# Second mixer of a hybrid encoder layer: where the next head's queries and keys are turned, when they are copied out, and reciprocals of two tiles at a time

## The chip, the cores and the metric

The kernel runs on one core of a Trainium2 chip. The metric is the time of one execution on the device, in microseconds (us), over the whole layer. A lower number is better. Three runs of the kernel before are shown, and one execution taken by the hardware profiler.

Engine names in the profile: PE is TensorE's matmul side, PEld its weight loads, DVE is VectorE, ACT is ScalarE, POOL is GpSimd, SP is SyncE, which issues the DMAs.

## The reference

One encoder layer over 2048 tokens of width 1024. The input projection feeds two mixers: A is grouped-query attention, B a dilated sliding-window attention with 8 heads of width 64. Their outputs are normalised, joined and projected; an MLP and a gated addition follow. The change lies in mixer B:

```
DILATED_PATTERNS = ((128, 1), (512, 4), (2048, 16))
    sc = einsum('brnqhd,brnkhd->brnqhk', qs, ks) * (HEAD_DIM ** -0.5)
    sc = where(valid, sc + bias, NEG_BIG)
    mx = max(sc, axis=-1)
    e = exp(sc - mx[..., None])
    den = sum(e, axis=-1)
    o = einsum('brnqhk,brnkhd->brnqhd', e, vs) / den[..., None]
```

The three patterns are merged by their softmax denominators. The kernel treats the union of the patterns' keys of a tile of queries as one softmax, with a table of biases that also holds the counts of keys that several patterns share and the masks.

## The kernel before

The layer is a chain of phases: projection, mixer A, mixer B (`mixer_b_phase`), and the feed phase with output projection, MLP and gate. Each phase is a block with its own program per engine, and a barrier stands between two. Semaphores order the engines inside a block; each engine runs its own program strictly as written, so the order in the code is the order of the work.

Mixer B loops over heads, two per turn of the hardware loop (`Fori`, `par` 0 and 1), and over NU = 16 tiles of 128 queries in each, n = 0 to 15. N counts tiles over all heads. Scores of a tile are 128 x 1024 at most: eight blocks of 128 keys, of which the first is left out where n mod 4 is 0 or 3, so that some tiles have seven. Every number is split in a high and a low float part for TensorE's faster float format, hence the pairs "hi" and "lo".

What one iteration N does on each engine:

- TensorE (from L1257): in iterations n = 2 to 9, `prepare(h + 1, n - 2)` (L1188): four transposes that turn one of eight blocks of the next head's queries or keys into the accumulator bank `out_acc[n % 2]`. Then `scores(N + 2)` (L1203, L1210, L1216), `turn(N + 1)` (L1226), which turns the probabilities, `fold_out(N + 1)` (L1248), which turns tile N - 1's sums back, and `values(N)` (L1240), which writes `out_acc[n % 2]`.
- ScalarE: `turned_hi(N + 1)` (L1307, two halves), `exponential(N + 2)` (L1300), in iterations n = 1 to 8 `pre_out(h + 1, n - 1)` (L1291), which copies the turned block out of its bank into `pre`, then `sums_out(N)` (L1313).
- VectorE: `add_bias(N + 2)` (L1362, three parts, and the maximum, L1365), `output` of tile N - 1 (L1382), which multiplies with the reciprocal of the denominator, `sums(N + 1)` (L1377), that reciprocal, and `turned_lo(N + 1)` (L1372, two halves).
- GpSimd: splits `pre` into high and low parts of the next head's queries and keys (`split_pre`, L1126 to L1133), adds parts of outputs (`summed`, L1148, L1153), splits the next head's values (`split_values`) and copies its bias tables (`tables`, L1104 to L1113), in this order.
- SyncE: loads of the next head's inputs and tables, stores of the outputs.

The waits that the change and the prediction speak of: `prepare` waits for `y_done`, which `output` raises, since it writes the bank that `output` of tile n - 2 has read. `values` waits for `y_done`, for `lo_done`, and in iterations 2 to 9 for `pre_raw`, which `pre_out` raises:

```
                pe.wait_ge(lo_done, N * 2 + 2)
                pe.wait_ge(y_done, N + 1)
                if 2 <= n < 2 + PRE:
                    pe.wait_ge(pre_raw, h * PRE + (n - 1))
```

`scores(N + 2)` waits only for `add_done` of tile N, whose bank it takes. `turn(N + 1)` waits for `exp_done`.

Of the kernel before, what the change touches and what calls it, by code (L numbers as in the profile page):

```python
# [969 lines left out]
def mixer_b_phase(nc, scr, step, ident, heads, feed, consts, chunks):  # L970
# [11 lines left out]
    SLOTS = 4  # L982
    with ExitStack() as ctx:
        k = Kit(nc, ctx, "mixb")
# [11 lines left out]
        den = k.sb("den", [P, SLOTS])  # L996
        rden = k.sb("rden", [P, SLOTS])
# [15 lines left out]
                                                                            "v_hi", "v_lo"))  # L1013
        sc_done, add_done, nm_done, exp_done = (k.sem(n) for n in ("sc_done", "add_done", "nm_done", "exp_done"))
        t_done, hi_done, lo_done, pv_done = (k.sem(n) for n in ("t_done", "hi_done", "lo_done", "pv_done"))
        rd_done, o_done, fold_done, y_done = (k.sem(n) for n in ("rd_done", "o_done", "fold_done", "y_done"))
        y_ready = k.sem("y_ready")
        y_out = k.sems("y_out", 2)
        QK_DMAS, V_DMAS = heads.QK_DMAS, heads.V_DMAS
# [1 line left out]
        PRE = 8  # L1021
# [156 lines left out]
        def _(pe):  # L1178
            def prepare(h, m):

                if m == 0:
                    pe.wait_ge(qk_dma, h * (16 * QK_DMAS) + 16 * QK_DMAS)
                first = isinstance(h, int)
                if first and m >= 6:
                    pe.wait_ge(pre_lo, m - 5)
                src = q_in if m < 4 else k_in
                for j in range(4):
                    mm = pe.transpose(pre_banks[m % (6 if first else 2)][:, j * P:(j + 1) * P],  # L1188
                                      src[:, 4 * (m % 4) + j, :], ident[:])
                mm.then_inc(pre_done, 1)  # L1190

            def scores(N, par, n):

                r, b = n // RES, n % RES
                if not (isinstance(N, int) and N < 2):
                    pe.wait_ge(add_done, N * 3 - 3)
                sc = score[n % 2]
                q = qT[par][:, n * P:(n + 1) * P]
                for part in range(2):
                    kt = kT[par][part]  # L1200
                    main = kt[:, PAD:PAD + S].rearrange("p (r m) -> p r m", r=RES)
                    own = first_own(n)
                    pe.matmul(sc[:, first_tile(n) * P:BANK], q, main[:, r, own * P:(own + RES - first_tile(n)) * P],  # L1203
                              start=part == 0, stop=part == 1)
                at = BANK
                runs = [x for x in ((0, r), (r + 1, RES)) if x[1] > x[0]]
                for a, z in runs:
                    for part in range(2):
                        main = kT[par][part][:, PAD:PAD + S].rearrange("p (r m) -> p r m", r=RES)
                        pe.matmul(sc[:, at:at + (z - a) * P], q, main[:, a:z, b * P:(b + 1) * P],  # L1210
                                  start=part == 0, stop=part == 1)
                    at += (z - a) * P
                for part in range(2):
                    t = kT[par][part][:, b * P:b * P + PAD]
                    ends = bass.AP(t.tensor, t.offset, [[SW, P], [SUB, RES], [P + PAD, 2], [1, PAD]])
                    mm = pe.matmul(sc[:, at:at + P], q, ends, start=part == 0, stop=part == 1)  # L1216
                mm.then_inc(sc_done, 1)

            def turn(N, n):
                pe.wait_ge(exp_done, N + 1)  # L1220
                for half in range(2):
                    if not (isinstance(N, int) and N == 0):
                        pe.wait_ge(lo_done, N * 2 + half - 1)
# [36 lines left out]
            with pe.Fori(0, NHB // 2) as it:  # L1260
                for par in range(2):
                    h = it * 2 + par
                    for n in range(NU):
                        N = h * NU + n
                        if 2 <= n < 2 + PRE:
                            pe.wait_ge(y_done, N + 1)
                            prepare(h + 1, n - 2)
                        if n < NU - 2:
                            scores(N + 2, par, n + 2)
                        else:  # L1270
                            if n == NU - 2:
                                pe.wait_ge(pre_lo, h * PRE + 2 * PRE)
                                pe.wait_ge(v_lo, h + 2)
                            scores(N + 2, 1 - par, n + 2 - NU)
                        turn(N + 1, (n + 1) % NU)
                        fold_out(N + 1, n - 1)
                        values(N, h, par, n)
            fold_out(NHB * NU + 1, NU - 1)

        @block.scalar  # L1280
        def _(act):
            def pre_hi_part(h, par, m):
                act.wait_ge(pre_done, h * PRE + m + 1)
                dst = qT[par][:, m * BANK:(m + 1) * BANK] if m < 4 else kT[par][0][:, PAD + (m - 4) * BANK:
                                                                               PAD + (m - 3) * BANK]
                act.activation(dst, pre_banks[m % 6], ACT.Copy).then_inc(pre_hi, 1)

            def pre_out(h, m):
                act.wait_ge(pre_done, h * PRE + m + 1)
                act.wait_ge(pre_lo, h * PRE + m - 1)  # L1290
                act.activation(pre[:, m % 2, :], out_acc[m % 2][:], ACT.Copy).then_inc(pre_raw, 1)  # L1291

            def value_hi(h, par):
                act.wait_ge(v_dma, h * (16 * V_DMAS) + 16 * V_DMAS)
                act.activation(v_hl[par][:, :, 0:HD], v_in[:], ACT.Copy).then_inc(v_hi, 1)

            def exponential(N, n):
                act.wait_ge(nm_done, N + 1)
                p = prob[:, n % SLOTS, first_tile(n) * P:]
                act.activation(p, p, ACT.Exp, bias=nmax[:, n % SLOTS:n % SLOTS + 1],  # L1300
                               accum_out=den[:, n % SLOTS:n % SLOTS + 1]).then_inc(exp_done, 1)

            def turned_hi(N, n):
                for half in range(2):
                    act.wait_ge(t_done, N * 2 + half + 1)
                    j = 0 if half else first_tile(n)
                    act.activation(pT[:, n % 2, 4 * half + j:4 * half + 4, 0, :],  # L1307
                                   turned[half][:, j * P:].rearrange("p (c n) -> p c n", n=P), ACT.Copy
                                   ).then_inc(hi_done, 1)

            def sums_out(N, n):
                act.wait_ge(pv_done, N + 1)
                act.activation(oT[:, n % 2, :], out_acc[n % 2][:, 0:2 * P], ACT.Copy).then_inc(o_done, 1)  # L1313

            for m in range(PRE):
                pre_hi_part(0, 0, m)
            exponential(0, 0)
            value_hi(0, 0)
            exponential(1, 1)
            turned_hi(0, 0)  # L1320
            with act.Fori(0, NHB // 2) as it:
                for par in range(2):
                    h = it * 2 + par
                    for n in range(NU):
                        N = h * NU + n
                        turned_hi(N + 1, n + 1)
                        exponential(N + 2, n + 2)
                        if 1 <= n < 1 + PRE:
                            pre_out(h + 1, n - 1)
                        sums_out(N, n)  # L1330

        @block.vector
        def _(ve):
# [38 lines left out]
                    ve.tensor_tensor(at[:, :, 1, :], turned[half][:, j * P:].rearrange("p (c n) -> p c n", n=P),  # L1372
                                     at[:, :, 0, :].bitcast(F32), ALU.subtract).then_inc(lo_done, 1)

            def sums(N, n):
                ve.wait_ge(exp_done, N + 1)
                ve.reciprocal(rden[:, n % SLOTS:n % SLOTS + 1], den[:, n % SLOTS:n % SLOTS + 1]).then_inc(rd_done, 1)  # L1377

            def output(count, n):

# [8 lines left out]
            add_bias(0, 0, 0)  # L1389
            add_bias(1, 0, 1)  # L1390
            value_lo(0, 0)
            sums(0, 0)
            turned_lo(0, 0)
            with ve.Fori(0, NHB // 2) as it:
                for par in range(2):
                    h = it * 2 + par
                    for n in range(NU):
                        N = h * NU + n
                        if n < NU - 2:
                            add_bias(N + 2, par, n + 2)  # L1400
                        else:
                            if n == NU - 2:
                                ve.wait_ge(t_done_pool, h * T_COPIES + 2 * T_COPIES)
                            add_bias(N + 2, 1 - par, n + 2 - NU)
                        if n % 2 == 1:
                            ve.wait_ge(y_ready, h * 16 + (n // 2 * 2 + 1))
                        output(N + 1, (n - 1) % NU)
                        sums(N + 1, n + 1)
                        turned_lo(N + 1, n + 1)
            output(NHB * NU + 1, NU - 1)  # L1410

# [805 lines left out]
```

## Time and profile before

| what | value |
|---|---|
| median of three runs | 3624.57 us (3621.48 to 3624.72) |
| profiled execution | 3623.18 us |
| its span, first to last instruction | 3621.4 us |
| mean granted TensorE clock | 0.975 of full speed |
| PE matmul / PEld busy over the span | 3418.6 (94%) / 2881.5 us (80%) |
| DVE / ACT / POOL busy | 2455.4 (68%) / 1892.9 (52%) / 2061.3 us (57%) |

The busy times are sums over all phases. Matmuls are pipelined and their ends are modelled, so a busy PE does not mean that it is at its peak. In a timeline, the distance between the starts of two neighbours on an engine is the step of the first; the duration may be longer, since neighbours overlap. The value in brackets is the idle time of the engine ahead of the instruction and what ended it.

### The profile page before, as it was taken

How to read it: one execution, taken by the hardware profiler on the slowest of the kernel's cores; microseconds unless marked ns; L12 is line 12 of the kernel's file. 1: busy time of each engine (PE TensorE's matmuls, PEld its weight loads, DVE VectorE, ACT ScalarE, POOL GpSimd, SP SyncE). 2: the span in 40 equal slices, each digit the busy share in tenths (PEclk: the TensorE clock that was granted, in tenths of full speed). 3: DMA queues.
4: the chain of work that ended last, by engine and by line, in shares of the span. 5: the costliest groups of instructions: out<-in, count | busy, mean ns of one | idle time of the engine just before them, and what ended most of it. 6: DMA issues, size and time to landing. Idle time of an engine off the chain costs nothing.

```text
span 3621.4 us, 55821 instructions
## 1 busy us (share of the span) xinstructions
PE 3418.6 (94%) x17910; PEld 2881.5 (80%) x17910; DVE 2455.4 (68%) x4319; ACT 1892.9 (52%) x3554; POOL 2061.3 (57%) x1416
## 2 busy tenths in 40 slices
PE   7999989999999899998699998999989999899997
PEld 6888868888888788888478886888868888778885
DVE  5555579999999788888355576555665556655554
ACT  3222268888888677777343353433543345433342
POOL 4555424443222265655467775677766777657773
PEclk9999989999999999999799999999999999999998
DMA  4545434443002233334234444444443444434441
GB/s 178 164 163 175 138 125 153 146 147 109 17 17 50 61 65 82 77 71 111 87 106 156 146 137 148 139 151 152 140 155 126 153 155 145 157 112 150 146 151 53
DMA packets 289135, 444.91 MB, mean 123 GB/s; under 512 B 175412, under 2 KB 194300, under 8 KB 282908
## 3 DMA queue, kind: packets, MB, share of 16 engines
q1 hardware_dynamic: 279580, 428.48, 38.0%
q10 hardware_dynamic: 9344, 13.73, 1.0%
q8 instruction: 119, 1.95, 0.2%
q14 instruction: 92, 0.75, 0.1%
HBM read 377.89 MB, written 76.71 MB: 126 GB/s over the span
## 4 chain that ended last, share of the span: by engine, by line
PE 42%; DVE 6%; ACT 2%; issue 1%; POOL 0%; DMA 0%; SPq 0%; DVEq 0%; ACTq 0%
PE feed_bank L1668 41%; DVE feed_res L1976 2%; DVE feed_total L1973 1%; DVE feed_xn L1949 1%; ACT feed_xT L1826 1%; PE feed_bank L1659 1%; DVE feed_xT L1958 0%; POOL feed_w_split L1619 0%; DVE feed_ms L1937 0%; DMA feed_y_in<-scr_yB 0%; DVE feed_total L2033 0%; DVE feed_rec L1940 0%; DVE feed_comb L2060 0%; ACT feed_junk L1801 0%; DVE feed_sums L2079 0%
## 5 line engine op out<-in xcount | busy, mean ns | idle before, releaser
L1619 POOL TENSOR_TENSOR feed_w_split<-feed_w_raw,feed_w_split 128x1024 fp32r<-128x1024 f32 x424 | 1077.9, 2551 | 254.6 <-ACT feed_w_split L1854 235.7
L1668 PE MATMUL feed_bank<-feed_w_split,feed_comb 128*128 128x512 f32 x3648 | 855.0, 395 | 28.0 <-DVE feed_sums L2079 10.4
L1668 PEld LDWEIGHTS feed_bank<-feed_w_split,feed_comb 128*128 128x128 f32 x3648 | 690.8, 190 | 181.2 <-DVE feed_sums L2079 12.9
L1668 PE MATMUL feed_bank<-feed_xT,feed_w_split 128*128 128x512 f32 x3072 | 700.7, 390 | 2.5 <-DVE feed_xT L1958 2.5
L1668 PEld LDWEIGHTS feed_bank<-feed_xT,feed_w_split 128*128 128x128 f32 x3072 | 577.5, 188 | 123.2 <-DVE feed_xT L1958 2.9
L1616 POOL TENSOR_SCALAR feed_w_split<-feed_w_raw 128x1024 fp32r<-128x1024 f32 x200 | 228.9, 1145 | 323.4 <-issue 306.5
L357 PE MATMUL proj_bank<-proj_w_split,proj_xT 128*128 128x512 f32 (+1 forms) x1920 | 402.5, 370 | 2.7 <-issue 2.7
L952 DVE TENSOR_TENSOR mixa_pT<-mixa_turned,mixa_pT 128x512 fp32r<-128x512 f32 x512 | 350.9, 685 | 58.4 <-ACT mixa_pT L898 50.1
L357 PEld LDWEIGHTS proj_bank<-proj_w_split,proj_xT 128*128 128x128 f32 x1920 | 333.3, 189 | 66.8 <-issue 5.6
L898 ACT ACTIVATE mixa_pT<-mixa_turned 128x512 fp32r<-128x512 f32 x512 | 307.1, 600 | 123.1 <-PE mixa_turned L836 104.1
L795 PE MATMUL mixa_out_acc<-mixa_pT,mixa_v_hl 128*128 128x512 f32 x1028 | 366.0, 437 | 0.7 <-DVE mixa_pT L952 0.7
L2033 DVE TENSOR_TENSOR feed_total<-feed_total,feed_bank 128x512 f32<-128x512 f32 x352 | 224.4, 681 | 195.7 <-PE feed_bank L1668 192.7
L1869 ACT ACTIVATE feed_rl<-feed_bank 128x512 f32<-128x512 f32 x128 | 76.5, 598 | 523.2 <-PE feed_bank L1668 523.2
L1854 ACT ACTIVATE feed_w_split<-feed_w_raw 128x1024 fp32r<-128x1024 f32 x224 | 236.6, 1065 | 189.8 <-PE feed_bank L1668 185.1
L923 DVE TENSOR_REDUCE mixa_nmax<-mixa_score 128x1 f32<-128x1024 f32 x264 | 322.0, 1221 | 14.3 <-PE mixa_score L782 7.7
L836 PE MATMUL mixa_turned<-layer_ident,mixa_prob 128*128 128x128 f32 x2048 | 307.7, 273 | 0.0
L836 PEld LDWEIGHTS mixa_turned<-layer_ident,mixa_prob 128*128 128x128 f32 x2048 | 253.1, 141 | 56.3 <-issue 0.2
L870 ACT ACTIVATE mixa_prob<-mixa_score,mixa_nmax 128x1024 f32<-128x1024 f32 x263 | 294.2, 1119 | 4.0 <-DVE mixa_nmax L923 4.0
L782 PE MATMUL mixa_score<-mixa_kT,mixa_qT 128*128 128x512 f32 x1056 | 289.1, 395 | 7.0 <-ACT mixa_prob L870 6.2
L2002 DVE TENSOR_TENSOR feed_comb<-feed_rl,feed_comb 128x256 fp32r<-128x256 f32 x128 | 154.0, 1203 | 174.5 <-ACT feed_comb L1873 174.2
L782 PEld LDWEIGHTS mixa_score<-mixa_kT,mixa_qT 128*128 128x128 f32 x1056 | 198.6, 189 | 55.8 <-ACT mixa_prob L870 8.7
L1668 PE MATMUL feed_bank<-feed_w_split,feed_xT 128*128 128x512 f32 x768 | 185.4, 402 | 9.5 <-ACT feed_total L1833 7.1
(198 smaller groups left out, 5101.9 us busy)
## 6 DMA issues: line engine op xcount, KB each, us to landing
feed_w_raw<-w_tail_dram SPq DMA_DIRECT2D x200, 512.0 KB, 3.6
feed_w_raw<-scr_wT SPq DMA_DIRECT2D x160, 512.0 KB, 3.3
proj_w_raw<-w_in_dram SPq DMA_DIRECT2D x39, 1024.0 KB, 5.2
feed_w_raw<-w_ff_dram SPq DMA_DIRECT2D x64, 512.0 KB, 3.5
scr_table<-scr_bias SPq DMA_DIRECT2D x8, 1520.0 KB, 9.0
proj_x_t<-x_dram SPq DMA_DIRECT2D x20, 512.0 KB, 5.8
mixa_q_in<-scr_qA SPq DMA_DIRECT2D x36, 256.0 KB, 3.4
mixb_q_in<-scr_qB SPq DMA_DIRECT2D x18, 512.0 KB, 5.7
```

Source lines behind the costliest of these rows:

```text
L357: mm = pe.matmul(acc[t][:, 0:width], xT[u][a][:, k0 + kk, t * P:(t + 1) * P], w[m][:, kk, :], start=first and kk == 0 and q == 0, stop=las ...
L782: mm = pe.matmul(score[:, at * BANK:(at + 1) * BANK], qT[g][:, h, :], kT[g][part][:, kc * BANK:(kc + 1) * BANK], start=part == 0, stop=par ...
L795: mm = pe.matmul(out_acc[half][:], v_hl[:, s, g, :], pT[part][:, s % NR, :], start=s % (NT // 2) == 0 and part == 0, stop=s % (NT // 2) == ...
L836: mm = pe.transpose(turned[s % 2][:, h * P:(h + 1) * P], prob[w][:, h, s * P:(s + 1) * P], ident[:])
L870: act.activation(prob[par][:, h, half * 2 * BANK:(half + 1) * 2 * BANK], score[:, 2 * (c % 2) * BANK:2 * (c % 2 + 1) * BANK], ACT.Exp, bia ...
L898: act.activation(pT[0][:, s % NR, :], turned[s % 2][:], ACT.Copy).then_inc(hi_done, 1)
L923: ve.tensor_reduce(nmax[:, par, c // G, c % G:c % G + 1], score[:, 2 * (c % 2) * BANK: 2 * (c % 2 + 1) * BANK], AXX, ALU.max, negate=True) ...
L952: ve.tensor_tensor(pT[1][:, s % NR, :], turned[s % 2][:], pT[0][:, s % NR, :].bitcast(F32), ALU.subtract).then_inc(lo_done, 1)
L1616: pool.tensor_scalar(w_sp[0][:, slot, :], w_raw[:, slot, :], 1.0, 0.0, ALU.mult, ALU.add).then_inc(w_hi, 1)
L1619: pool.tensor_tensor(w_sp[1][:, slot, :], w_raw[:, slot, :], w_sp[0][:, slot, :].bitcast(F32), ALU.subtract).then_inc(w_lo, 1)
L1668: mm = pe.matmul(dst, lhs, rhs, start=start, stop=stop)
L1854: act.activation(w_sp[0][:, slot, :], w_raw[:, slot, :], ACT.Copy).then_inc(w_hi_ff, 1)
```

## The change

Three edits, all in `mixer_b_phase`. On TensorE `prepare` and its wait for `y_done` move behind `scores(N + 2)`, in the same iterations. On ScalarE `pre_out` moves from the place between `exponential` and `sums_out` to the head of the following iteration, ahead of `turned_hi`. On VectorE the reciprocal is taken for two tiles at a time, in even iterations, and the one ahead of the loop and its semaphore `rd_done`, for which nobody waited, go.

```diff
@@ TensorE's loop
                     for n in range(NU):
                         N = h * NU + n
-                        if 2 <= n < 2 + PRE:
-                            pe.wait_ge(y_done, N + 1)
-                            prepare(h + 1, n - 2)
                         if n < NU - 2:
                             scores(N + 2, par, n + 2)
                         else:
@@
                             scores(N + 2, 1 - par, n + 2 - NU)
+                        if 2 <= n < 2 + PRE:
+                            pe.wait_ge(y_done, N + 1)
+                            prepare(h + 1, n - 2)
                         turn(N + 1, (n + 1) % NU)
@@ ScalarE's loop
+                        if 2 <= n < 2 + PRE:
+                            pre_out(h + 1, n - 2)
                         turned_hi(N + 1, n + 1)
                         exponential(N + 2, n + 2)
-                        if 1 <= n < 1 + PRE:
-                            pre_out(h + 1, n - 1)
                         sums_out(N, n)
@@ VectorE
-            def sums(N, n):
+            def sums_of_two(N, n):
+
+                at = slice(n % SLOTS - 1, n % SLOTS + 1)
                 ve.wait_ge(exp_done, N + 1)
-                ve.reciprocal(rden[:, n % SLOTS:n % SLOTS + 1], den[:, n % SLOTS:n % SLOTS + 1]).then_inc(rd_done, 1)
+                ve.reciprocal(rden[:, at], den[:, at])
@@
-            sums(0, 0)
             turned_lo(0, 0)
@@ VectorE's loop
-                        sums(N + 1, n + 1)
+                        if n % 2 == 0:
+                            sums_of_two(N + 1, n + 1)
                         turned_lo(N + 1, n + 1)
```

TensorE, the iteration n = 8 of the first head of a loop turn (`mixb_k_in` is the next head's keys, `mixb_prob` the probabilities, `mixb_oT` the sums to be turned back). Before:

```order
L1188 MATMUL mixb_out_acc<-layer_ident,mixb_k_in 128x128 x4
L1196 ISA
L1203 MATMUL mixb_score<-mixb_kT,mixb_qT 128x512 x2
L1210 MATMUL mixb_score<-mixb_kT,mixb_qT 128x256 x2
L1210 MATMUL mixb_score<-mixb_kT,mixb_qT 128x128 x2
L1216 MATMUL mixb_score<-mixb_kT,mixb_qT 128x128 x2
L1223 ISA
L1226 MATMUL mixb_turned<-layer_ident,mixb_prob 128x128 x8
L1248 MATMUL mixb_out_acc<-layer_ident,mixb_oT 128x128 x2
L1235 REGISTER_ALU
L1238 REGISTER_ALU
L1240 MATMUL mixb_out_acc<-mixb_pT,mixb_v_hl 128x256 x7
```

The same iteration in the changed kernel:

```order
L1196 ISA
L1203 MATMUL mixb_score<-mixb_kT,mixb_qT 128x512 x2
L1210 MATMUL mixb_score<-mixb_kT,mixb_qT 128x256 x2
L1210 MATMUL mixb_score<-mixb_kT,mixb_qT 128x128 x2
L1216 MATMUL mixb_score<-mixb_kT,mixb_qT 128x128 x2
L1188 MATMUL mixb_out_acc<-layer_ident,mixb_k_in 128x128 x4
L1223 ISA
L1226 MATMUL mixb_turned<-layer_ident,mixb_prob 128x128 x8
L1248 MATMUL mixb_out_acc<-layer_ident,mixb_oT 128x128 x2
L1235 REGISTER_ALU
L1238 REGISTER_ALU
L1240 MATMUL mixb_out_acc<-mixb_pT,mixb_v_hl 128x256 x7
```

The four transposes of L1188 stood ahead of the scores and now stand between the scores and the turning.

ScalarE, a `prepare` iteration in the middle of a head. Between two exponentials, before:

```order
L1300 ACTIVATE mixb_prob,mixb_den<-mixb_prob,mixb_nmax 128x1024
L1289 REGISTER_ALU
L1291 ACTIVATE mixb_pre<-mixb_out_acc 128x512
L1313 ACTIVATE mixb_oT<-mixb_out_acc 128x256
L1305 ISA
L1307 ACTIVATE mixb_pT<-mixb_turned 128x4x128
```

And now:

```order
L1300 ACTIVATE mixb_prob,mixb_den<-mixb_prob,mixb_nmax 128x1024
L1313 ACTIVATE mixb_oT<-mixb_out_acc 128x256
L1289 REGISTER_ALU
L1291 ACTIVATE mixb_pre<-mixb_out_acc 128x512
L1305 ISA
L1307 ACTIVATE mixb_pT<-mixb_turned 128x4x128
```

The copy L1291 has changed places with L1313; it now stands directly ahead of the first half of the turned probabilities.

## Rows read from the trace of the kernel before

**Rows 1.** Windows of mixer B, their sum: TensorE matmuls, loads, VectorE, ScalarE, GpSimd.

```profile
sum 463.00, PE 433.36 PEld 408.16 DVE 392.51 ACT 357.56 POOL 257.87; mean PE 108.34 PEld 102.04 DVE 98.13 ACT 89.39 POOL 64.47
```

**Rows 2.** Waits of TensorE's weight loads, 1250 to 1712: us, times, longest.

```profile
PEld mixb_out_acc L1188 <- DVE mixb_y_part L1382: 26.2, 56, 0.9
...
PEld mixb_out_acc L1188 <- issue: 1.0, 3, 0.3
```

**Rows 3.** Timeline, TensorE, n = 8: start, us, engine, line, what, [idle before].

```profile
1517.52 0.66 PE L1188 MATMUL mixb_out_acc<-layer_ident,mixb_k_in 128*128 128x128 f32 x4 [0.41 <-DVE mixb_y_part L1382]
1517.93 0.70 PE L1203 MATMUL mixb_score<-mixb_kT,mixb_qT 128*128 128x512 f32 x2
...
1519.10 1.06 PE L1226 MATMUL mixb_turned<-layer_ident,mixb_prob 128*128 128x128 f32 x8
1520.00 0.38 PE L1248 MATMUL mixb_out_acc<-layer_ident,mixb_oT 128*128 128x128 f32 x2
1520.13 1.08 PE L1240 MATMUL mixb_out_acc<-mixb_pT,mixb_v_hl 128*128 128x256 f32 x7
1521.48 0.66 PE L1188 MATMUL mixb_out_acc<-layer_ident,mixb_k_in 128*128 128x128 f32 x4 [0.27 <-DVE mixb_y_part L1382]
```

**Rows 4.** Timeline, VectorE, the same iteration.

```profile
1519.46 0.69 DVE L1362 CUSTOM_DVE_ANT_0 mixb_prob<-mixb_score,mixb_t_own 128x512 f32<-128x512 f32 x1 [0.87 <-PE mixb_score L1216]
...
1520.95 0.47 DVE L1382 TENSOR_SCALAR mixb_y_part<-mixb_out_acc,mixb_rden 128x256 f32<-128x256 f32 x1
1521.35 0.15 DVE L1377 RECIPROCAL mixb_rden<-mixb_den 128x1 f32<-128x1 f32 x1
1521.42 1.27 DVE L1372 TENSOR_TENSOR mixb_pT<-mixb_turned,mixb_pT 128x512 fp32r<-128x512 f32 x2
```

**Rows 5.** Timeline, VectorE, iterations n = 12 to 14, first bias of each.

```profile
1532.54 0.68 DVE L1362 CUSTOM_DVE_ANT_0 mixb_prob<-mixb_score,mixb_t_own 128x512 f32<-128x512 f32 x1
...
1535.68 0.56 DVE L1362 CUSTOM_DVE_ANT_0 mixb_prob<-mixb_score,mixb_t_own 128x384 f32<-128x384 f32 x1
...
1538.84 0.56 DVE L1362 CUSTOM_DVE_ANT_0 mixb_prob<-mixb_score,mixb_t_own 128x384 f32<-128x384 f32 x1
```

**Rows 6.** Timeline, TensorE, turning of iteration n = 12.

```profile
1532.49 1.09 PE L1226 MATMUL mixb_turned<-layer_ident,mixb_prob 128*128 128x128 f32 x8 [0.35 <-ACT mixb_prob L1300]
```

**Rows 7.** Timeline, first `prepare` of a head: TensorE, ScalarE, GpSimd.

```profile
1493.99 0.65 PE L1188 MATMUL mixb_out_acc<-layer_ident,mixb_q_in 128*128 128x128 f32 x4
...
1494.76 0.60 ACT L1291 ACTIVATE mixb_pre<-mixb_out_acc 128x512 f32<-128x512 f32 x1 [0.16 <-PE mixb_out_acc L1188]
...
1495.56 0.62 POOL L1126 TENSOR_SCALAR mixb_qT<-mixb_pre 128x512 fp32r<-128x512 f32 x1 [4.35 <-ACT mixb_pre L1291]
```

**Rows 8.** Timeline, TensorE behind ScalarE's last copy.

```profile
1714.37 0.36 ACT L1313 ACTIVATE mixb_oT<-mixb_out_acc 128x256 f32<-128x256 f32 x1
...
1714.78 0.44 PE L1248 MATMUL mixb_out_acc<-layer_ident,mixb_oT 128*128 128x128 f32 x2 [1.43 <-ACT mixb_oT L1313]
```

**Rows 9.** Timeline, ScalarE, iteration n = 8.

```profile
1519.76 1.09 ACT L1307 ACTIVATE mixb_pT<-mixb_turned 128x512 fp32r<-128x512 f32 x2 [0.68 <-PE mixb_turned L1226]
1521.07 1.15 ACT L1300 ACTIVATE mixb_prob<-mixb_prob,mixb_nmax 128x1024 f32<-128x1024 f32 x1 [0.22 <-DVE mixb_nmax L1365]
...
1522.22 0.58 ACT L1291 ACTIVATE mixb_pre<-mixb_out_acc 128x512 f32<-128x512 f32 x1
1522.70 0.37 ACT L1313 ACTIVATE mixb_oT<-mixb_out_acc 128x256 f32<-128x256 f32 x1
```

**Rows 10.** Timeline, GpSimd, the last copy of the next head's tables.

```profile
1535.06 0.24 POOL L1113 COPY mixb_t_end<-mixb_t_near 128x64 f32<-128x64 f32 x1
```

**Rows 11.** Instructions on the reciprocals' tile: ns min/median/max, first and last start.

```profile
L1377 DVE RECIPROCAL mixb_rden<-mixb_den x129: 151/154/157, 1252.9 to 1713.5; 128x1 f32<-128x1 f32 x129
```

**Rows 12.** Timeline, ScalarE, the first work of the next phase.

```profile
1719.76 0.63 ACT L1817 ACTIVATE feed_junk<-feed_total 128x512 bf16<-128x512 f32 x1 [5.02 <-PEq L983]
```

More of the change, by code:

```diff
@@ L1015, in mixer_b_phase @@
         t_done, hi_done, lo_done, pv_done = (k.sem(n) for n in ("t_done", "hi_done", "lo_done", "pv_done"))
-        rd_done, o_done, fold_done, y_done = (k.sem(n) for n in ("rd_done", "o_done", "fold_done", "y_done"))
+        o_done, fold_done, y_done = (k.sem(n) for n in ("o_done", "fold_done", "y_done"))
         y_ready = k.sem("y_ready")
```

## The prediction

> **What bounds the kernel now.** I read the stretches of time first. Mixer B runs from about 1250 to 1713 us of the 3621.4 us span. In these 463 us TensorE's matmuls are busy 433, VectorE 393, ScalarE 358 and GpSimd 258 [rows 1]: TensorE is the fullest, VectorE the next. Nothing outside this stretch is touched.
>
> Then the waits of TensorE's weight loads there [rows 2]. The largest is ahead of L1188, `prepare`, the turning of the next head's queries and keys: 26.2 us in 56 waits for VectorE's `output` (L1382), and 1.0 us in 3 more laid to issue. There are 64 `prepare` in the loop (8 heads, 8 each), so 59 of 64 wait, 0.46 us each.
>
> The timeline shows why. One iteration of n = 8 on TensorE [rows 3]: `prepare` starts at 1517.52, scores 1517.93, turning 1519.10, folding 1520.00, values 1520.13, next `prepare` 1521.48, a period of 3.96. VectorE starts on those scores at 1519.46, 0.36 after TensorE went on to turning; it had been idle 0.87 before [rows 4]. It reaches `output` at 1520.95, ends it at 1521.42, and TensorE starts the next `prepare` 0.06 later. So a loop closes in these iterations: scores, bias, output, `prepare`, next scores. Both engines idle in it. `prepare` needs that output only because it writes the accumulator bank that the output reads; the scores behind it need nothing of it.
>
> In the other 8 iterations of a head there is no `prepare`. VectorE starts at 1532.54, 1535.68 and 1538.84, 3.14 and 3.16 apart [rows 5], nearly without a gap. There VectorE sets the pace, now and then the exponential: one turning waits 0.35 for it [rows 6].
>
> **The change part by part.**
>
> *Scores ahead of `prepare`.* Scores may start when values are issued. `prepare` then comes 1.17 later (the scores' step, 1517.93 to 1519.10 [rows 3]). Is the output ready by then? It ends 0.36 + 1.49 + 0.47 = 2.32 after the end of the scores before (1519.10 to 1519.46, to 1520.95, to its end [rows 3, 4]); the next `prepare` comes one period, some 3.6, after that. Slack 1.3. The wait goes whole. Not all of it is idle time: the seven value matmuls take (1.08 - 0.28)/6 = 0.133 each, so they are issued by 1520.13 + 0.93 = 1521.06, and the 0.42 to 1521.48 stands in the trace as 0.47 of the load unit's idle time. I take 0.03 off each: 27.2 - 59 x 0.03 = 25.4 us gained. The work of such an iteration is then 3.96 - 0.44 = 3.52.
>
> *A wait that takes its place.* `values` waits for `pre_raw`, the copy of the turned block out of the bank (L1291 on ScalarE), since it writes that bank. Before, scores lay between `prepare` and `values`; now only turning and folding do. Counted from the start of `prepare`: the copy starts 0.77 later when ScalarE is waiting for it (1493.99 to 1494.76), takes 0.60 [rows 7], and its end is seen after 0.05 (TensorE behind L1313: 1714.37 + 0.36 to 1714.78 [rows 8]) to 0.20 (GpSimd: 1495.36 to 1495.56 [rows 7]). Values can start at 1.42 to 1.57. TensorE is there at 0.41 + 0.90 + 0.13 = 1.44 (the steps of `prepare`, turning and folding) with eight blocks to turn [rows 3], and some 0.11 earlier in the half of the iterations with seven. The stall is 0 to 0.13 with eight and 0.09 to 0.24 with seven: 0.045 to 0.185 on average. I take 0.07, near the low end, because the row with 0.05 is TensorE's own wait for ScalarE. 64 x 0.07 = 4.5 us lost (bounds 2.9 and 12).
>
> This is where a rule and the rows part. The Trainium skill ("TensorE: Matmul & The Clock Gate", step-by-step phases) says that TensorE pulls weight loads ahead of matmuls in flight. Read as reaching across a semaphore wait, it would hide the restart and bring this stall to about nothing. The rows speak against that reach: behind a wait the loads idle at least as long as the matmuls (26.2 us of load idle time stands before L1188 [rows 2]).
>
> *The copy ahead of the turned probabilities.* ScalarE now does copy, two `turned_hi`, exponential, `sums_out`. The copy starts at 0.77 and holds the engine 0.48 (1522.22 to 1522.70 [rows 9]), so `turned_hi` starts at 1.25. Without it, it would start at 0.41 + 0.66 = 1.07 (1519.10 to 1519.76 [rows 3, 9]). It is 0.18 late, some 0.3 with seven blocks. Who waits? The exponential follows at 1.25 + 1.09 = 2.34; its input is ready at about 0.36 + 1.61 = 1.97 (1519.46 to 1521.07 [rows 4, 9]). It is done at 2.34 + 1.15 = 3.49, and the next turning wants it at 3.6 + 0.41 = 4.0. `turned_lo` ends near 3.7 and is wanted at 5.0. `sums_out` frees ScalarE at 3.9, and the next copy starts at 4.3. All have slack, the least about 0.4, so I cost this at nothing. When that cover is gone each 0.1 us is 6.4 us.
>
> *GpSimd and the queues.* The splits of the copied blocks begin about 1.1 us later in an iteration. The next head's tables are behind them on GpSimd: their last copy ends at 1535.30 [rows 10], while VectorE wants them at 1538.84 [rows 5]. 3.5 us of slack become some 2.4. Nothing, and SP's loads start as much later with a whole half head to land.
>
> *Reciprocals of two tiles.* Of 129 L1377 [rows 11] 65 go, one of them ahead of the loop. Each is 0.15 long, but its step is 0.07 (1521.35 to 1521.42 [rows 4]): 4.5 us less VectorE work. Half of it falls in `prepare` iterations, where VectorE idles. Of the other 2.2 us a part goes to the waits for the exponential. I take 1.0 (bounds 0 and 4.5).
>
> *Behind the mixer.* The next phase starts behind the last store, at 1719.76, after an idle time that ends at the barrier [rows 12]. It shifts with the mixer.
>
> **Sum.** 25.4 - 4.5 + 1.0 = 21.9 us. The profiled execution took 3623.18, so 3601.3; the median of the three runs, 3624.57, is 1.4 above it: **3602.7 us**.
>
> **The rivals.**
>
> *The new wait is hidden too.* Stall zero, reciprocals paid to 2.2: 27.6 us, 3597 us. For it: with eight blocks TensorE arrives at 1.44 against 1.42. Against: with seven it arrives early by any of the rows. Chance 0.10. The rule on pulled loads, above, would lead here.
>
> *ScalarE's order takes the gain.* If `turned_hi` is on the path after all, 0.18 to 0.3, say 0.23, comes on each of 64 iterations: 14.7 us, 7.2 left, 3617 us. For it: a period near 3.6 rests on four hand-overs whose slack is 0.4. Against: the walk above. Chance 0.10. The Trainium skill (same page, on queue depths) calls ScalarE's queue a strict FIFO, so nothing passes a copy that waits; if the copy waited for `prepare` longer than I count, this rival is how it would show.
>
> *VectorE is the bound in these iterations too*, so that nearly nothing is won: its work is 3.14 to 3.16 [rows 5] against 3.6, so it would need a slip of 0.5. 3624 us. Chance 0.04.
>
> *Slower: the copy comes late.* TensorE stands at `values` with all next scores queued behind it. ScalarE is in order, so the copy starts only when the exponential and `sums_out` of the iteration before are through, at 3.9 against 4.3. It decides from 0.4 of slip on, and the change loses once the stall passes 0.42 per iteration, the wait removed. With a slip of 0.9, a stall of 0.57: 64 x 0.57 = 36 lost against 26 won, 3635 us. For it: the copy is now first in ScalarE's iteration. Against: ScalarE is busy only 358 of 463 us [rows 1]. Chance 0.04.
>
> **Numbers.** The forecast has 0.72. What a measurement of this kernel can tell from no change is about 0.2%, 7 us. Range: bounds give 25.4 - 2.9 + 4.5 = 27 at best (3597.6) and 25.4 - 12 = 13.4 at worst (3611.2). I widen it to 3596 to 3613 for the first rival and part of the second. Faster by over 0.2%: 0.72 + 0.10 + half of the second rival = 0.87. Within: 0.09. Slower: 0.04.
>
> **What would show it.** Right: no wait of L1188 for L1382 left; a new small wait of L1240 for L1291, under 0.25 each, longer where seven blocks are turned; VectorE starts 3.5 to 3.7 apart in `prepare` iterations and near 3.1 in the others; mixer B shorter by 20 to 24 us, all else shifted. Wrong: waits of L1240 over 0.3; turning waiting for the exponential in `prepare` iterations; VectorE without idle time there; or a tail that does not shift.

## The result, and the profile after

The changed kernel takes 3593.44 us (four runs, 3591.33 to 3594.26) against 3623.53 us (four runs) before: a ratio of 0.9917, 95% interval 0.9899 to 0.9934. That is 30.1 us less. The direction and the wait that goes were forecast; the size was not, nor that the forecast new wait would stay away. 21.9 us were expected, and the time lies 2.6 us below the range. The profiled execution took 3593.50 us.

The head of the page of the changed kernel, and the line of TensorE's granted clock over the 40 slices:

```profile
span 3591.7 us, 55756 instructions
...
PE 3406.2 (95%) x17910; PEld 2881.9 (80%) x17910; DVE 2454.1 (68%) x4254; ACT 1878.5 (52%) x3554; POOL 2058.2 (57%) x1416
...
PEclk9999989999999999998799999999999999999998
```

The clock is as before (0.974 on average against 0.975). The instructions are the same but for 65 reciprocals. The sum over mixer B, the window 1250 to 1682:

```profile
sum 432.00, PE 417.95 PEld 405.96 DVE 391.33 ACT 344.32 POOL 256.94; mean PE 417.95 PEld 405.96 DVE 391.33 ACT 344.32 POOL 256.94
```

Set beside [rows 1], 463 us have become 432 with the same work in them but for the reciprocals: VectorE's busy time fell by 1, the weight loads' by 2. Idle time went, and a few steps of TensorE became shorter (told with why the prediction was wrong). Two busy figures fell by more, and neither by less work. ScalarE's fell by 13, while its instructions last as long as before (L1307 571 ns on average against 570, L1291 599 against 589): records that follow each other closely overlap, as 1500.25 + 0.60 and 1500.75 below, and the overlap counts once. TensorE's fell by 15; it is made of modelled ends, and a group is drawn longer behind a wait (L1188 0.66 in [rows 3], 0.62 below), which explains some of it; the rest was not taken apart.

All waits of TensorE's weight loads of 1 us and more, from 1250 to 1685, so that the last folding of the mixer is in (us, times, longest). They answer to [rows 2]:

```profile
PEld mixb_score L1203 <- issue: 7.6, 3, 2.8
PEld mixb_turned L1226 <- issue: 6.0, 24, 0.3
PEld mixb_turned L1226 <- DVE mixb_v_hl L1347: 4.8, 1, 4.8
PEld mixb_out_acc L1248 <- ACT mixb_oT L1313: 1.6, 1, 1.6
PEld mixb_turned L1226 <- DVE mixb_pT L1372: 1.0, 2, 0.5
```

No row of L1188 for L1382 is left, and no row of L1240 for L1291 has come. The first was forecast; the second was not: the view lists no wait of `values` for the copy. One iteration n = 8 on TensorE, the counterpart of [rows 3]:

```profile
1498.50 0.62 PE L1203 MATMUL mixb_score<-mixb_kT,mixb_qT 128*128 128x512 f32 x2
...
1499.59 0.62 PE L1188 MATMUL mixb_out_acc<-layer_ident,mixb_k_in 128*128 128x128 f32 x4
1500.05 1.04 PE L1226 MATMUL mixb_turned<-layer_ident,mixb_prob 128*128 128x128 f32 x8
1500.93 0.38 PE L1248 MATMUL mixb_out_acc<-layer_ident,mixb_oT 128*128 128x128 f32 x2
1501.06 1.08 PE L1240 MATMUL mixb_out_acc<-mixb_pT,mixb_v_hl 128*128 128x256 f32 x7
1501.98 0.51 PE L1203 MATMUL mixb_score<-mixb_kT,mixb_qT 128*128 128x384 f32 x2
```

The order is scores, `prepare`, turning, folding, values. The period is 1498.50 to 1501.98, 3.48 instead of 3.96. ScalarE beside it, the counterpart of [rows 9]:

```profile
1499.37 0.39 ACT L1313 ACTIVATE mixb_oT<-mixb_out_acc 128x256 f32<-128x256 f32 x1
1500.25 0.60 ACT L1291 ACTIVATE mixb_pre<-mixb_out_acc 128x512 f32<-128x512 f32 x1 [0.50 <-PE mixb_out_acc L1188]
1500.75 1.08 ACT L1307 ACTIVATE mixb_pT<-mixb_turned 128x512 fp32r<-128x512 f32 x2
1501.70 1.16 ACT L1300 ACTIVATE mixb_prob<-mixb_prob,mixb_nmax 128x1024 f32<-128x1024 f32 x1
...
1502.83 0.39 ACT L1313 ACTIVATE mixb_oT<-mixb_out_acc 128x256 f32<-128x256 f32 x1
```

The copy L1291 starts 0.66 after `prepare`, ends at 1500.85, and the values start at 1501.06. The two turned halves (L1307) start 0.70 behind the turning, where it was 0.66 before ([rows 3, 9]: 1519.10 to 1519.76) with eight blocks; with seven it is 0.70 against 0.55. So they are late by 0.04 and 0.15, forecast were 0.18 and 0.3, and TensorE's steps show nobody waiting for that.

VectorE's first bias at the ends of one run of `prepare` iterations and one run without. After, iterations n = 10, then n = 2, then n = 10 of the next head:

```profile
1506.70 0.56 DVE L1362 CUSTOM_DVE_ANT_0 mixb_prob<-mixb_score,mixb_t_own 128x384 f32<-128x384 f32 x1 [0.23 <-PE mixb_score L1216]
...
1531.45 0.56 DVE L1362 CUSTOM_DVE_ANT_0 mixb_prob<-mixb_score,mixb_t_own 128x384 f32<-128x384 f32 x1 [0.22 <-PE mixb_score L1216]
...
1558.82 0.56 DVE L1362 CUSTOM_DVE_ANT_0 mixb_prob<-mixb_score,mixb_t_own 128x384 f32<-128x384 f32 x1 [0.23 <-PE mixb_score L1216]
```

Before, n = 9, n = 1 and n = 9. The run begins one iteration earlier there because `prepare` stood ahead of the scores:

```profile
1523.32 0.56 DVE L1362 CUSTOM_DVE_ANT_0 mixb_prob<-mixb_score,mixb_t_own 128x384 f32<-128x384 f32 x1 [0.63 <-PE mixb_score L1216]
...
1548.06 0.55 DVE L1362 CUSTOM_DVE_ANT_0 mixb_prob<-mixb_score,mixb_t_own 128x384 f32<-128x384 f32 x1
...
1579.00 0.56 DVE L1362 CUSTOM_DVE_ANT_0 mixb_prob<-mixb_score,mixb_t_own 128x384 f32<-128x384 f32 x1 [0.63 <-PE mixb_score L1216]
```

Eight iterations with `prepare`: 1531.45 to 1558.82, 27.37 us, against 30.94 (1548.06 to 1579.00). That is 3.42 for one, a little under the 3.5 to 3.7 that the prediction named as its sign. Eight without: 24.75 against 24.74. So it is 3.57 us per head where `prepare` is, and nothing elsewhere. Eight heads make 28.6; a further 1.5 us come from four `prepare` iterations in the whole mixer that took 0.37 longer than their like before (4.23 from values to values against 3.86) and no longer do.

The next phase starts at 1688.98 instead of 1719.76 [rows 12], 30.8 earlier. The profiled executions as a whole differ by 29.7, so about 1 us of that is lost again behind the mixer:

```profile
1688.98 0.63 ACT L1819 ACTIVATE feed_junk<-feed_total 128x512 bf16<-128x512 f32 x1 [5.03 <-PEq L983]
```

### The profile page after: what moved, and what is told of

Same layout as the page of the kernel before. It is cut to its first block, busy times and chain, and to the rows that moved or that the text cites. A ratio compares the mean times of both kernels' runs of the same rounds, so it can differ in the third digit from the quotient of the medians.

```text
span 3591.7 us, 55756 instructions
## 1 busy us (share of the span) xinstructions
PE 3406.2 (95%) x17910; PEld 2881.9 (80%) x17910; DVE 2454.1 (68%) x4254; ACT 1878.5 (52%) x3554; POOL 2058.2 (57%) x1416
## 4 chain that ended last, share of the span: by engine, by line
PE 42%; DVE 6%; ACT 2%; issue 1%; POOL 0%; DMA 0%; SPq 0%; DVEq 0%; ACTq 0%
PE feed_bank L1670 42%; DVE feed_res L1978 2%; DVE feed_total L1975 1%; DVE feed_xn L1951 1%; ACT feed_xT L1828 1%; PE feed_bank L1661 1%; DVE feed_xT L1960 0%; POOL feed_w_split L1621 0%; DVE feed_ms L1939 0%; DMA feed_y_in<-scr_yB 0%; DVE feed_rec L1942 0%; DVE feed_total L2035 0%; DVE feed_comb L2062 0%; ACT feed_junk L1803 0%; DVE feed_sums L2081 0%
```

## The experiments

Theory A: the wait of `prepare` for the output is the whole gain, and the swap on ScalarE only keeps a new wait away. The rivals: B, ScalarE has slack enough for either order; C, the swap gains by itself; D, the reciprocals explain what came over the forecast. The first four kernels take the parts one by one, each against the kernel before. A run's name stands in brackets at its result, and it is used further down.

### Only `prepare` behind the scores

```diff
@@ kernel before, TensorE's loop
-                        if 2 <= n < 2 + PRE:
-                            pe.wait_ge(y_done, N + 1)
-                            prepare(h + 1, n - 2)
@@ behind scores(N + 2, ...)
+                        if 2 <= n < 2 + PRE:
+                            pe.wait_ge(y_done, N + 1)
+                            prepare(h + 1, n - 2)
```

> Only prepare moves behind the scores on TensorE; ScalarE's order and the reciprocals stay as before. Theory A (the removed wait for the output is the whole gain, and the swap on ScalarE only keeps a new wait away): the copy now waits for prepare with the copy of the sums (L1313) queued behind it, so folding (L1248) stalls. From the changed kernel's trace the copy starts 0.66 after prepare; 0.66 + 0.48 + 0.38 + 0.05 = 1.57 against a folding that is due 1.22 to 1.34 after prepare: 0.23 to 0.35 in each of 64 iterations, 15 to 22 us. Expected 3608 to 3616, prepare iterations about 3.7 apart. Rival B (ScalarE has slack enough for either order): 3593 to 3596, no wait of L1248.

Measured (e_pe): 3625.44 us against 3624.13, ratio 1.0002 (0.9993 to 1.0012). All of the gain is gone, which is more than either theory gave: theory A had 3608 to 3616. The wait in question, TensorE's loads ahead of folding, from 1250 to 1680 (24.9 us in 64 waits over the whole mixer):

```profile
PEld mixb_out_acc L1248 <- ACT mixb_oT L1313: 23.1, 59, 0.5
```

Iteration n = 8, TensorE, then the two copies on ScalarE:

```profile
1518.49 0.62 PE L1188 MATMUL mixb_out_acc<-layer_ident,mixb_k_in 128*128 128x128 f32 x4
1518.95 1.04 PE L1226 MATMUL mixb_turned<-layer_ident,mixb_prob 128*128 128x128 f32 x8
1520.07 0.44 PE L1248 MATMUL mixb_out_acc<-layer_ident,mixb_oT 128*128 128x128 f32 x2
1520.37 1.09 PE L1240 MATMUL mixb_out_acc<-mixb_pT,mixb_v_hl 128*128 128x256 f32 x7
1521.29 0.51 PE L1203 MATMUL mixb_score<-mixb_kT,mixb_qT 128*128 128x384 f32 x2
```

```profile
1519.15 0.60 ACT L1291 ACTIVATE mixb_pre<-mixb_out_acc 128x512 f32<-128x512 f32 x1 [1.03 <-PE mixb_out_acc L1188]
1519.64 0.38 ACT L1313 ACTIVATE mixb_oT<-mixb_out_acc 128x256 f32<-128x256 f32 x1
```

The copy of the turned block (L1291) starts 0.66 after `prepare`, the copy of the sums (L1313) stands behind it and ends at 1520.02, and folding starts at 1520.07. It was due at 1518.95 + 0.88 = 1519.83. That is the 0.24 that theory A expected here. But folding itself then takes 1520.07 to 1520.37, 0.30, where it takes 0.13 in the stream (1500.93 to 1501.06 above). So the wait costs 0.41 here, not 0.24. Over all 64 `prepare` iterations the step of the turning is 1.14 on average against 0.82 in the changed kernel, 0.32 more, and that of folding 0.32 against 0.14, 0.18 more. 64 x 0.50 = 32 us, and the two kernels differ by 3625.44 - 3593.44 = 32.0. Theory A thus had the first part right and lacked the second. Rival B falls: ScalarE's order decides.

### Only the swap on ScalarE

```diff
@@ kernel before, ScalarE's loop
+                        if 2 <= n < 2 + PRE:
+                            pre_out(h + 1, n - 2)
                         turned_hi(N + 1, n + 1)
                         exponential(N + 2, n + 2)
-                        if 1 <= n < 1 + PRE:
-                            pre_out(h + 1, n - 1)
                         sums_out(N, n)
```

> Only the copy moves on ScalarE, which in fact swaps it with the copy of the sums (L1313) and nothing else; TensorE's order as before. Theory A: nobody waits for either in this place, so no change, 3621 to 3626. Rival C (part of the 30 us comes from ScalarE releasing the sums earlier): 3610 to 3618.

Measured (e_act): 3624.07 against 3624.13 us, ratio 1.0000 (0.9990 to 1.0010). The wait for the output stands as it did, up to 1680 us (before, up to there, 24.8 in 53):

```profile
PEld mixb_out_acc L1188 <- DVE mixb_y_part L1382: 24.5, 52, 0.9
```

Rival C falls. Each of the two moves alone is worth nothing, and together they are worth 30 us.

### Only the reciprocals

The edit is the third part of the change, on the kernel before.

> Only the reciprocals of two tiles at a time. Theory A: at most the half of 4.5 us that falls where VectorE sets the pace, so 3621.5 to 3624.5, and the eight iterations without prepare 24.6 to 24.8 us together against 24.8. Rival D (the reciprocals explain what came over the forecast): 3616 to 3620.

Measured (e_recip): 3621.14 against 3624.13 us, ratio 0.9995 (0.9985 to 1.0005): not told apart from no change (the ratio of the two medians is 0.9992, within the interval too). The output's wait is a little smaller, up to 1680 us (before 24.8 in 53):

```profile
PEld mixb_out_acc L1188 <- DVE mixb_y_part L1384: 23.3, 53, 0.6
```

The 1.5 us between them are the four longer iterations named above: they are gone here too (the last section comes back to them).

### Both moves without the reciprocals

The first two parts of the change on the kernel before.

> Both moves without the reciprocals. Theory A: within 1.5 us of the changed kernel, 3593 to 3596. Rival D: 3597 to 3600.

Measured (e_pe_act): 3594.08 us, ratio 0.9916 (0.9899 to 0.9932). It was run once more beside the changed kernel on one chip:

> The changed kernel once more, beside the other two on one chip: 3591 to 3595.

> The two moves without the reciprocals once more, beside the changed kernel on one chip. In the earlier traces the eight iterations without prepare took 24.83 us against 24.74 with the reciprocals, so 0.7 us over the changed kernel, which the times can hardly show; 2 us or more would mean that the reciprocals act elsewhere too.

Measured (a_after, e_norecip): 3592.28 us (ratio 0.9914, 0.9900 to 0.9927) with the reciprocals of two, 3593.30 us (0.9918, 0.9905 to 0.9932) without. The difference of 1.0 us is within the scatter. Rival D falls: the reciprocals bring at most about 1 us here, and the runs cannot tell it from nothing.

### The copy behind the turned probabilities

```diff
@@ changed kernel, ScalarE's loop
-                        if 2 <= n < 2 + PRE:
-                            pre_out(h + 1, n - 2)
                         turned_hi(N + 1, n + 1)
+                        if 2 <= n < 2 + PRE:
+                            pre_out(h + 1, n - 2)
```

> The changed kernel with the copy behind the two turned_hi instead of ahead of them. If values (L1240) truly waits for the copy, it starts 1.04 (when turned_hi starts) + 1.0 = 2.0 to 2.1 after prepare instead of 0.66, ends at 2.7, and values, due at 1.36 to 1.46, stalls 1.25 each: some 80 us, 3670 to 3680. If something else releases the bank earlier, or ScalarE's order does not matter: under 3600.

Measured (e_copy_late): 3675.24 us in one run, within the range, against 3622.71 before and 82 above the changed kernel's 3593.44. The wait that the forecast had feared is now there, up to 1680 us (78.2 in 64 over the whole mixer):

```profile
PEld mixb_out_acc L1240 <- ACT mixb_pre L1291: 67.1, 55, 1.2
```

So the dependence is real, and the place ahead of `turned_hi` is needed.

### The copy twice

```diff
@@ changed kernel, pre_out; spare is a tile of its own
+                act.activation(spare[:], out_acc[m % 2][:], ACT.Copy)
                 act.activation(pre[:, m % 2, :], out_acc[m % 2][:], ACT.Copy).then_inc(pre_raw, 1)
```

> The changed kernel with the turned block copied twice, first into a spare tile, then as before: the copy's end comes 0.48 later. In the changed kernel the copy ends 1.26 after prepare and values starts at 1.36 to 1.46 without a wait in the trace. With the doubled copy it ends at 1.74. If the end is seen after 0.05, the stall is 1.79 less 1.41 = 0.38 on average, 24 us, about 3618; if after 0.20, 0.53, 34 us, about 3628. If ScalarE's own queue becomes the bound as well, more than that. No change would mean that the copy is not what values waits for.

Measured (e_copy_twice): 3621.81 us in one run, 28.4 above the changed kernel's 3593.44 (forecast 24 or 34). The wait over the whole mixer, 0.39 each (forecast 0.38 for the hand-over of 0.05):

```profile
PEld mixb_out_acc L1241 <- ACT mixb_pre L1293: 24.7, 64, 0.5
```

An iteration with seven blocks, TensorE, then ScalarE:

```profile
1513.60 0.62 PE L1189 MATMUL mixb_out_acc<-layer_ident,mixb_k_in 128*128 128x128 f32 x4
1514.06 0.93 PE L1227 MATMUL mixb_turned<-layer_ident,mixb_prob 128*128 128x128 f32 x7
1514.82 0.38 PE L1249 MATMUL mixb_out_acc<-layer_ident,mixb_oT 128*128 128x128 f32 x2
1515.40 1.11 PE L1241 MATMUL mixb_out_acc<-mixb_pT,mixb_v_hl 128*128 128x256 f32 x7 [0.19 <-ACT mixb_pre L1293]
```

```profile
1514.26 0.60 ACT L1292 ACTIVATE mixb_spare<-mixb_out_acc 128x512 f32<-128x512 f32 x1 [0.71 <-PE mixb_out_acc L1189]
1514.76 0.59 ACT L1293 ACTIVATE mixb_pre<-mixb_out_acc 128x512 f32<-128x512 f32 x1
```

The second copy ends at 1514.76 + 0.59 = 1515.35 and values starts at 1515.40: a hand-over of 0.05. Without a wait it would have started 0.13 to 0.14 after folding, at 1514.96. The second copy starts 0.50 behind the first (1514.76 against 1514.26), which stands where the changed kernel has its only one, and the stall is 0.44. So with seven blocks the changed kernel passes this wait with some 0.06 to spare. It is hidden, and only just; with eight blocks the turning takes 0.11 more and the margin is that much wider. No sign was found that ScalarE became a bound of its own.

### `prepare` spread over the head

In the changed kernel TensorE sets the pace where `prepare` is and VectorE where it is not. Two kernels mix them.

```diff
@@ changed kernel; banks now by n % 2, and every test of n by this list
+        AT = (0, 2, 3, 5, 7, 8, 10, 12)
-                        if 2 <= n < 2 + PRE:
+                        if n in AT:
```

GpSimd's `split_values` goes ahead of the first split, and its tables behind the third.

> The changed kernel with the eight prepare of a head not in iterations 2 to 9 but in 0, 2, 3, 5, 7, 8, 10 and 12, and GpSimd's splitting of the values and its tables earlier in the head, so that they are still in time. Theory: the iterations with prepare are bound by TensorE (3.42 apart), those without by VectorE and by the chain scores, bias, exponential, turning (3.09 apart), while TensorE's own work there is about 2.9. Mixed, TensorE's 8 x 3.42 + 8 x 2.9 = 50.6 us per head is the bound against 52.1 now: up to 12 us less, 3582 to 3588. Rival: the chain scores to turning holds in each single iteration without prepare whatever its neighbours do, then no change (3592 to 3595); or the shorter time for the next loads or GpSimd's queue costs, then slower.

Measured (e_spread): 3597.82 us (3594.50 to 3601.41), ratio 0.9933 (0.9917 to 0.9950), so no gain over the changed kernel: the 3582 to 3588 of the theory are missed. GpSimd's splits, now behind its longer work, hold up the copy, and `values` with it:

```profile
1428.96 0.60 ACT L1299 ACTIVATE mixb_pre<-mixb_out_acc 128x512 f32<-128x512 f32 x1 [1.83 <-POOL mixb_qT L1131]
...
1429.61 0.90 PEld L1248 LDWEIGHTS mixb_out_acc<-mixb_pT,mixb_v_hl 128*128 128x128 f32 x7 [1.04 <-ACT mixb_pre L1299]
```

The second kernel takes `AT = (1, 3, 4, 6, 7, 9, 10, 12)`, the values behind the second split and the tables behind the fourth.

> As e_spread, with prepare in iterations 1, 3, 4, 6, 7, 9, 10 and 12 and GpSimd's work in another order (values behind the first two splits, tables behind the fourth), so that it holds up no copy. Undisturbed heads of e_spread took 51.7 us against 52.1 of the changed kernel. Theory: each iteration has its own bound whatever its neighbours, so 8 x 0.4 = 3 us less than the changed kernel at best, 3589 to 3594, beside it. Rival: the mixed order leaves slack that GpSimd's pile-ups had hidden, 3580 to 3587.

Measured (e_spread2), beside the changed kernel's 3592.28 us: 3588.81 us (3586.84 to 3589.90), ratio to before 0.9902 (0.9887 to 0.9917). It is the fastest kernel of this study by median, 3.5 us under the changed one, close to the 3 us that the theory of a bound per iteration gives (the median lies 0.2 under its range). In the traces an undisturbed head takes 51.6 us against 52.1, from values to values. The two intervals against before overlap, so the step from the changed kernel is likely and not settled. The hoped-for 12 us of e_spread did not come in either kernel.

## Why the prediction was right and wrong

**The wait for the output goes whole: right.** No wait of L1188 is left, and e_pe_act keeps the whole gain.

**A wait takes its place, 4.5 us: wrong.** This is the step that failed most: the stall of `values` on the copy (L1240 on L1291). Forecast 4.5 us, measured about 0.2. The forecast took 0.77 from `prepare` to the copy, from one row [rows 7], and that row is the first `prepare` of a head. This is the changed kernel in the same place, iteration n = 2:

```profile
1531.09 0.62 PE L1188 MATMUL mixb_out_acc<-layer_ident,mixb_q_in 128*128 128x128 f32 x4
...
1531.83 0.60 ACT L1291 ACTIVATE mixb_pre<-mixb_out_acc 128x512 f32<-128x512 f32 x1 [0.75 <-PE mixb_out_acc L1188]
...
1532.48 1.22 PE L1240 MATMUL mixb_out_acc<-mixb_pT,mixb_v_hl 128*128 128x256 f32 x8
```

There the copy comes 0.74 behind `prepare`, and `values` starts 0.05 behind its end, 1.39 behind `prepare`. Folding's step is 0.16 there and 0.14 elsewhere, so some 0.03 of the forecast stall is real in this one iteration of each head. In the other seven the copy comes after 0.66, in the changed kernel, in e_pe and in e_copy_twice alike. With 0.66 + 0.60 + 0.05 = 1.31 its end is seen before the 1.36 at which TensorE arrives with seven blocks (0.46 + 0.76 + 0.14). The trace before already held rows that spoke against 0.77 as the rule, one iteration behind [rows 7]:

```profile
1497.72 0.66 PE L1188 MATMUL mixb_out_acc<-layer_ident,mixb_q_in 128*128 128x128 f32 x4
...
1498.41 0.60 ACT L1291 ACTIVATE mixb_pre<-mixb_out_acc 128x512 f32<-128x512 f32 x1
```

The copy starts 0.69 after its `prepare`, with no idle time of ScalarE ahead of it, so the block is ready after 0.69 at the latest. Why the first block of a head is 0.08 later than the others stays open; whether the remaining 0.03, between 0.77 and 0.74, comes from a `prepare` that begins on a wait is not shown. The hand-over of 0.05, the low end of the two bounds, was right. e_copy_late shows that the dependence is as described, and e_copy_twice that 0.06 is left.

**25.4 us for the wait removed: right, 24.8.** That is what the steps of `values` ahead of the 64 `prepare` lost, added up over both traces from start to start (87.4 us before, 62.6 after). The 0.03 that the prediction took off each wait did not follow from its row, where 0.47 of load idle time stood for 0.42 (0.05, which would make 24.3).

**The steps of the neighbours: a term that the forecast had at nothing.** For n = 8 the idle time was put at 0.44, and the period fell by 0.48: scores take 1.09 behind values (1498.50 to 1499.59) against 1.17 behind `prepare` [rows 3], `prepare` 0.46 against 0.41, turning 0.88 against 0.90. Over all 64 iterations the steps of scores, `prepare` and turning together lost 3.6 us (scores -5.2, turning -1.5, `prepare` +3.1). The forecast moved a step and took it that its neighbours' steps stay as they were.

**Reciprocals, 1.0 us: consistent**, and too small to be measured. In the medians it is 0.6 and 1.0.

**Together.** From the first values to the last, 453.9 us before and 423.7 after, mixer B lost 30.2 us: 24.8 of wait and 3.6 of neighbours' steps, less 0.2 of new wait, and 2.0 in the iterations without `prepare`, the reciprocals' share among them; the rest of this last part was not taken apart. Against the forecast the new wait is worth +4.3, the neighbours +3.6, this last part +1.0 over the reciprocals' 1.0, and the removed wait -0.6: 21.9 + 8.3 = 30.2, against 30.1 in the medians. With the stall as its only error the forecast would still have had the time inside its range (25.4 + 1.0 = 26.4 us, 3598); the neighbours' steps took it out.

**The rivals.** The one that came true is that the new wait is hidden too, and it had a chance of 0.10. ScalarE's order did not take the gain, VectorE was not the bound, and the copy did not come late.

**The copy ahead of the turned probabilities costs nothing: right, and more than that.** The turned halves were late by less than forecast. The prediction treated this move as a part to be cleared of cost. It did not ask what `prepare`'s move does without it. e_pe gives the answer: 32 us over the changed kernel, the whole gain. The swap moves L1313 out from behind a copy that now waits for TensorE. The prediction's list of waits looked at the new order only, and never asked who waits for `sums_out` in the old one.

**VectorE's pace without `prepare`: right.** 24.75 against 24.74 us, and 3.20 and 3.16 for the iterations n = 12 and 13.

**The tail shifts: right**, 30.8 us at the start of the next phase.

**The rule on weight loads** (the Trainium skill, "TensorE: Matmul & The Clock Gate", step-by-step phases: loads are pulled ahead of matmuls in flight). The reading that would hide the stall pointed at the better number, 26.4 (25.4 + 1.0), but not by its reason. In e_copy_twice, where `values` does stall on the copy, its matmuls start 0.05 behind the copy's end and its first weight load at 1515.39, 0.01 ahead of them, so the loads do not hide that wait. In the changed kernel there is next to no stall for them to hide.

## What to carry to other kernels

Two moves may each be worth nothing and together be worth the whole: when a producer on one engine moves back in its iteration, look at what is queued behind its consumer on the other, and move that ahead. Take the distance from a producer to its consumer from several rows of the trace, not from the first of its kind: here the first of each head was 0.08 longer than the other seven, and a copy that started later without waiting gave a bound. When a group moves, let its neighbours' steps have a range too. A stall that is forecast from hundredths of a microsecond has zero inside its range, so keep the range open on that side.

## What the runs showed of the hardware

A wait on TensorE can cost more than its own length. In e_pe two transposes ahead of the value matmuls take 0.29 to 0.30 from start to next start in most iterations in which they begin on a wait (in 15 of the 64 it is 0.33 to 0.46), and 0.13 to 0.14 in the stream. What happens in the 0.16 was not tried. Behind the doubled copy the value matmuls themselves show nothing like it: seven of them take 1515.40 to 1516.34, 0.94, against 0.92.

In the iteration n = 8 the same eight score matmuls take 1.17 us from start to next start behind four transposes and 1.09 behind value matmuls, while the transposes' own step grows from 0.41 to 0.46. Which property of the neighbour ahead or behind does this stays open.

Before the change, four `prepare` iterations took 0.37 us longer than their like, each time at the same place, n = 5 of the first head of a loop turn. They are absent in the changed kernel. In e_recip, which only takes instructions out of VectorE's program, they are absent too. In e_pe_act, with the reciprocals as before, VectorE still slips there (its first biases stand 3.77 apart against 3.38 in the second head), but it makes this up in the next two iterations, and TensorE's steps show nothing. So the slip goes with VectorE's program with the single reciprocals, and the two moves hide it. Its cause was not tried.
